# Feed-forward gate and up products with high and low rows as one 512-column operand, and a third of the modulation rows in the second block

## The reference

```python
h = x                                            # first_block, DEPTH = 2
for layer in range(2):
    h = h + mixer(rms_norm(h, mix_norm[layer]))  # layer 0: gated linear recurrence; layer 1: stick-breaking attention
    z = rms_norm(h, ffn_norm[layer])
    gu = z @ ffn_w_in[layer]                     # (256, 1024) @ (1024, 2 * 2816)
    h = h + (silu(gu[:, :2816]) * gu[:, 2816:]) @ ffn_w_out[layer]
x = rms_norm(h, final_norm)
# second_block
mod = silu(c) @ w_ada + b_ada                    # 6 vectors of 1024: shifts, scales, gates
x = x + g1 * attentions(rmsnorm(x) * (1 + sc1) + sh1)
x = x + g2 * mixture_of_32_experts(rmsnorm(x) * (1 + sc2) + sh2)
out = rmsnorm(x)
```

## Time and profile before

| | |
|---|---|
| median of 3 runs | 1275.25 us (1275.18 to 1276.27) |
| the profiled execution, span from first to last instruction | 1277.6 us |
| mean granted clock of PE | 0.953 |
| PE busy | 1116.7 us (87% of the span), 9331 matmuls |
| DVE busy | 685.3 us (54%) |
| ACT busy | 421.0 us (33%) |
| DMA | 362.48 MB, mean 284 GB/s |

### The profile page before, as it was taken

One profiled execution on the slowest core, in us unless ns is written; L12 is line 12 of the kernel. 1 busy time (PEld: TensorE's weight loads), 2 busy tenths in 40 slices (PEclk: granted clock), 3 DMA queues, 4 the chain that ended last, 5 costly groups with the idle time before them and its releaser, 6 DMA issues.

```text
span 1277.6 us, 23118 instructions
## 1 busy us (share of the span) xinstructions
PE 1116.7 (87%) x9331; PEld 904.2 (71%) x9333; DVE 685.3 (54%) x1069; ACT 421.0 (33%) x532; POOL 32.8 (3%) x71
## 2 busy tenths in 40 slices
PE   9999999999999999999999999678766567666676
PEld 8999999999968999999998899533322233322232
DVE  5799988887445746557866767632112112112114
ACT  3775333345384433334644673410000000000001
POOL 0000000000000000001000000000000000000000
PEclk9999999999999999999999999889888888888889
DMA  9678988874530785550463336799999999999996
GB/s 347 225 262 301 342 299 302 305 261 158 176 128 1 263 311 198 173 174 2 179 225 132 133 141 239 305 378 416 428 427 430 427 428 430 427 430 427 428 430 259
DMA packets 99401, 362.48 MB, mean 284 GB/s; under 512 B 4160, under 2 KB 51664, under 8 KB 84112
## 3 DMA queue, kind: packets, MB, share of 16 engines
q1 hardware_dynamic: 95216, 335.06, 68.0%
q0 software_dynamic: 3984, 26.50, 5.3%
q10 hardware_dynamic: 144, 0.10, 0.0%
HBM read 360.58 MB, written 1.06 MB: 283 GB/s over the span
## 4 chain that ended last, share of the span: by engine, by line
PE 60%; DMA 23%; DVE 10%; ACT 3%; issue 2%; another core or an unknown queue 1%; SPq 0%; POOLq 0%; DVEq 0%; POOL 0%; ACTq 0%
DMA wbuf<-in_w_up 22%; PE ps L1897 16%; PE ps L1820 9%; PE ps L1783 8%; PE ps L2231 6%; PE ps L2107 4%; DVE parts L1107 3%; PE ps L1804 3%; PE ps L1829 2%; PE ps L2251 1%; PE ps L2281 1%; PE ps L1773 1%; PE ps L2014 1%; PE ps L1980 1%; DMA wbuf<-in_ffn_w_in 1%
## 5 line engine op out<-in xcount | busy, mean ns | idle before, releaser
L2231 PE MATMUL ps<-wbuf,big 128*32 128x256 f32 x2176 | 166.2, 470 | 109.4 <-DMA wbuf<-in_w_up 97.8
L1897 PE MATMUL ps<-big_parts,parts 128*128 128x256 f32 x2112 | 255.0, 282 | 1.4 <-DVE parts L1107 1.4
L1107 DVE TENSOR_TENSOR parts<-wbuf,parts 128x2048 fp32r<-128x2048 f32 x92 | 208.7, 2287 | 84.8 <-ACT parts L835 43.9
L1897 PEld LDWEIGHTS ps<-big_parts,parts 128*128 128x128 f32 x2112 | 252.3, 188 | 2.2 <-DVE parts L1107 1.4
L2231 PEld LDWEIGHTS ps<-wbuf,big 128*32 128x32 f32 x2176 | 85.5, 134 | 203.8 <-issue 98.1
L1693 DVE TENSOR_TENSOR big<-big,ps 128x128 f32<-128x128 f32 x33 | 9.5, 288 | 265.2 <-ACT big L1039 265.2
L1039 ACT ACTIVATE big<-ps 128x128 f32<-128x128 f32 x33 | 9.2, 278 | 415.7 <-PE ps L2231 415.7
L1820 PE MATMUL ps<-big_parts,parts 128*128 128x256 f32 x1088 | 132.9, 282 | 0.6 <-DVE parts L1107 0.6
L1820 PEld LDWEIGHTS ps<-big_parts,parts 128*128 128x128 f32 x1088 | 130.7, 189 | 0.8 <-DVE parts L1107 0.8
L1783 PE MATMUL ps<-parts_f,parts 128*128 128x256 f32 x704 | 98.4, 284 | 0.0
L1783 PEld LDWEIGHTS ps<-parts_f,parts 128*128 128x128 f32 x704 | 90.5, 192 | 0.1
(11 more groups left out here) (353 smaller groups left out, 1409.9 us busy)
## 6 DMA issues: line engine op xcount, KB each, us to landing
wbuf<-in_w_down SPq DMA_DIRECT2D x32, 2048.0 KB, 37.9
wbuf<-in_w_gate SPq DMA_DIRECT2D x31, 2048.0 KB, 32.6
wbuf<-in_w_up SPq DMA_DIRECT2D x31, 2048.0 KB, 37.1
wbuf<-in_ffn_w_in SPq DMA_DIRECT2D x44, 1024.0 KB, 12.1
wbuf<-in_w_ada POOLq DMA_DIRECT2D x24, 1024.0 KB, 8.6
wbuf<-in_ffn_w_out SPq DMA_DIRECT2D x22, 1024.0 KB, 5.1
wbuf<-in_w_in SPq DMA_DIRECT2D x10, 2048.0 KB, 8.8
wbuf<-in_attn_w_qkv SPq DMA_DIRECT2D x6, 2048.0 KB, 8.6
```

Of the source, the lines that this page charges most:

```text
L1107: nc.vector.tensor_tensor(lo, whole, hi.bitcast(F32), ALU.subtract).then_inc(done, 1)
L1897: ins = mm(ps[:, b, d * 256:(d + 1) * 256], w[pw][:, k, d * P:(d + 1) * P], h_part_of[px][:, k], start=(k == 0 and d == 0 and i == 0), sto ...
L2231: ins = mm(at, rows, gu_place[s][:, :, k, r * P:(r + 1) * P], start=(k == 0), stop=(k == KC - 1))
```

## The change

1. `half` makes two matmuls for each k and d instead of three. The first has the high weights and a moving operand of 512 columns, the 256 high and the 256 low rows of the same chunk (`h_both`, one access pattern over both regions). The second has the low weights and the 256 high rows. A column group d now has a bank of its own, with the sum of two products in its left half and the product with the low rows in its right half. Gate has banks 0 and 1 in every step, up has 2 and 3.
2. ACT copies the right halves to SBUF (`copy_low`), DVE adds the left halves to them (`sum_of_parts`) and then scales the sum from SBUF to SBUF. PE waits for the sum of the step before when it writes the banks again. In a step ACT copies gate's right halves first (in step 0 of a stage behind the split of the next gate weights and the norm root), and up's after silu.
3. The norm's sums of squares use bank 5 instead of 3.
4. Units 0 to 15 of the modulation stay in `ffn(0)`, one or two at a step (`ADA_FROM`). The other 16 rows of 128 x 1024 are loaded one by one by POOL into a free region of `big` once `wo1` is used, and `ffn(1)` takes two of them at the end of each step from 1 to 8 (`ada_row`). The row `c_row` is loaded and activated a second time. The small instructions that make the gains stand behind step 8 of `ffn(1)`. "ada" is free after 16 units.

```diff
 WARM_UP = 20
-SUM_BANK = (7, 3, 5, 3, 3, 2, 0, 4)
+SUM_BANK = (7, 5, 5, 5, 3, 2, 0, 4)
...
-ADA_FROM = tuple(range(2, ADA_UNITS - 1, 2))
+ADA_FIRST = 16
+ADA_ROWS = ADA_GROUP * (ADA_UNITS - ADA_FIRST)
+ADA_FROM = (2, 3, 5, 6, 8, 9, 10, 12, 13, 15, ADA_FIRST)
 
...
         X_AT_FFN = WORK + 2080
         h_part_of = [big_parts[:, X_AT_FFN + i * 2048:X_AT_FFN + (i + 1) * 2048].rearrange("p (k t) -> p k t", k=KC) for i in range(2)]
+        h_both = big_parts[:, X_AT_FFN:X_AT_FFN + 4096].rearrange("p (i k t) -> p k i t", i=2, k=KC)
...
-                eng.wait_ge(ada_used, ADA_UNITS)
+                eng.wait_ge(ada_used, ADA_FIRST)
             elif name == "qm":
...
+            for u in range(ADA_FIRST):
                 if u >= 2:
                     pool.wait_ge(ada_used, u - 1)
                 pool.dma_start(ada_place[u % 2], a["w_ada_2"][:, ADA_GROUP * u:ADA_GROUP * (u + 1), :]).then_inc(ada_loaded[u % 2], 16)
+            pool.wait_ge(o_done, KC)
+            pool.dma_start(c_row, a["c_2"].to_broadcast([P, D])).then_inc(c_in, 16)
+            wait_used(pool, "wo1")
+            for r in range(ADA_ROWS):
+                if r >= 2:
+                    pool.wait_ge(ada_used, ADA_FIRST + r - 1)
+                pool.dma_start(ada_row_place[r % 2], a["w_ada_2"][:, ADA_GROUP * ADA_FIRST + r]).then_inc(ada_loaded[r % 2], 16)
 
             pool.wait_ge(mod_ready, 2)
...
 
+                def copy_low(dst, b):
+                    nc.scalar.activation(dst.rearrange("p (d t) -> p d t", d=2), ps[:, b:b + 2, SEQ:], ACT.Copy).then_inc(ffn_copied, 1)
+
                 def step(s, n, loads, next_loads, before=True):
 
+                    act.wait_ge(ffn_g, n + 1)
+                    if before:
+                        copy_low(hid[:, s], 0)
                     if next_loads is not None:
-                        act.wait_ge(ffn_g, n + 1)
                         split_g(1 - s, next_loads)
                         if not before:
                             norm_root(2 * layer + 1)
+                            copy_low(hid[:, s], 0)
                     else:
-                        act.wait_ge(ffn_g, n + 1)
                         act.wait_ge(fo_loaded[s], 16 * loads)
                         nc.scalar.activation(fd_part_last[0], ffn_views(s)[2], ACT.Copy).then_inc(fd_hi, 1)
                         if layer:
                             hi_unit("km")
-                    act.wait_ge(ffn_gate_scaled, n + 1)
+                    act.wait_ge(ffn_gate_scaled, 2 * n + 2)
                     nc.scalar.activation(hid[:, s], hid[:, s], ACT.Silu).then_inc(ffn_silu, 1)
                     act.wait_ge(ffn_gu, n + 1)
+                    if before:
+                        act.wait_ge(ffn_hid, 4 * n)
+                    copy_low(up_scaled, 2)
                     if next_loads is None:
                         hi_unit("qm" if layer else "q0")
...
                 step(0, base, ffn_loads(layer, 0), ffn_loads(layer, 1), before=False)
+                if layer:
+                    act.wait_ge(c_in, 32)
+                    nc.scalar.activation(c_row, c_row, ACT.Silu).then_inc(silu_c, 1)
...
+            def ada_row(unit, r):
+                w = ada_row_place[r]
+                dve.wait_ge(ada_loaded[r], unit * 16 + 16 * (ADA_FIRST // 2 + 1))
+                at = unit * ADA_GROUP + (ADA_GROUP * ADA_FIRST + r)
+                nc.vector.scalar_tensor_tensor(out=w, in0=w, scalar=1.0, in1=c_row, op0=ALU.mult, op1=ALU.mult, accum_out=ada[:, bass.ds(at, 1)]).then_inc(ada_used, 1)
+
             def ada_unit(u):
...
 
+            def modulation():
...
+                def sum_of_parts(dst, b):
+                    return nc.vector.tensor_tensor(by_token(dst), ps[:, b:b + 2, 0:SEQ], by_token(dst), ALU.add)
+
                 def scale_gate(s, n):
-                    dve.wait_ge(ffn_g, n + 1)
-                    nc.vector.tensor_tensor(by_token(hid[:, s]), by_token(ps[:, 2 * s, :]), root, ALU.mult).then_inc(ffn_gate_scaled, 1)
-
-                def step(s, n, following=True, first=False):
+                    dve.wait_ge(ffn_copied, 2 * n + 1)
+                    sum_of_parts(hid[:, s], 0).then_inc(ffn_gate_scaled, 1)
+                    dve.wait_ge(ffn_gate_scaled, 2 * n + 1)
+                    nc.vector.tensor_tensor(by_token(hid[:, s]), by_token(hid[:, s]), root, ALU.mult).then_inc(ffn_gate_scaled, 1)
+
+                def step(s, n, following=True, first=False, unit=None):
                     if first:
...
-                    dve.wait_ge(ffn_gu, n + 1)
-                    nc.vector.tensor_tensor(by_token(up_scaled), by_token(ps[:, 2 * s + 1, :]), root, ALU.mult).then_inc(ffn_hid, 1)
-                    dve.wait_ge(ffn_hid, 2 * n + 1)
+                    dve.wait_ge(ffn_copied, 2 * n + 2)
+                    sum_of_parts(up_scaled, 2).then_inc(ffn_hid, 1)
+                    dve.wait_ge(ffn_hid, 4 * n + 1)
+                    nc.vector.tensor_tensor(by_token(up_scaled), by_token(up_scaled), root, ALU.mult).then_inc(ffn_hid, 1)
+                    dve.wait_ge(ffn_hid, 4 * n + 2)
                     dve.wait_ge(ffn_silu, n + 1)
                     nc.vector.tensor_tensor(hid[:, s], hid[:, s], up_scaled, ALU.mult).then_inc(ffn_hid, 1)
...
-                    nc.vector.tensor_copy(hid_part[s][0], hid[:, s]).then_inc(ffn_hid_hi, 1)
-                    subtract(hid_part[s][1], hid[:, s], hid_part[s][0], ffn_hid_hi, n + 1, ffn_hid_lo)
+                    dve.wait_ge(ffn_hid, 4 * n + 3)
+                    nc.vector.tensor_copy(hid_part[s][0], hid[:, s]).then_inc(ffn_hid, 1)
+                    subtract(hid_part[s][1], hid[:, s], hid_part[s][0], ffn_hid, 4 * n + 4, ffn_hid_lo)
                     if following:
                         split_u(1 - s, n + 1)
                         subtract(fd_part[1], ffn_views(s)[2], fd_part[0], fd_hi, n + 1, fd_lo)
...
                         for u in range(ADA_FROM[n], ADA_FROM[n + 1]):
                             ada_unit(u)
+                    if unit is not None:
+                        for r in range(ADA_GROUP):
+                            ada_row(unit, r)
 
                 if layer == 0:
                     for n in range(FFN_STEPS):
                         step(n % 2, n, following=n + 1 < FFN_STEPS, first=n == 0)
                     return
                 step(0, base, first=True)
+                dve.wait_ge(silu_c, 2)
                 with dve.Fori(0, (FFN_STEPS - 3) // 2) as j:
-                    step(1, 2 * j + base + 1)
-                    step(0, 2 * j + base + 2)
+                    step(1, 2 * j + base + 1, unit=2 * j)
+                    step(0, 2 * j + base + 2, unit=2 * j + 1)
+                modulation()
                 step(1, base + FFN_STEPS - 2)
                 step(0, base + FFN_STEPS - 1, following=False)
 
             ffn(0)
             add_and_lower(lambda b: add_bank(f"ffn0_{FFN_STEPS - 1}", b), 2, xq_part, lambda k: col(R_MIX + KC + k), FH_ATT, False)
-            ada_unit(ADA_UNITS - 1)
 
...
                         for d in range(2):
-                            for i, (px, pw) in enumerate(PART_PAIRS):
-                                ins = mm(ps[:, b, d * 256:(d + 1) * 256], w[pw][:, k, d * P:(d + 1) * P], h_part_of[px][:, k],
-                                         start=(k == 0 and d == 0 and i == 0), stop=(k == KC - 1 and i == 2), skip_group_check=True)
+                            columns = slice(d * P, (d + 1) * P)
+                            mm(ps[:, b + d, :], w[0][:, k, columns], h_both[:, k], start=(k == 0), stop=False, skip_group_check=True)
+                            ins = mm(ps[:, b + d, 0:SEQ], w[1][:, k, columns], h_part_of[0][:, k], start=False, stop=(k == KC - 1), skip_group_check=True)
                     return ins
 
-                def gate_up(slot, step, between=None, wait_rows=False):
+                def gate_up(step, between=None, wait_rows=False, evacuated=True):
                     pe.wait_ge(fg_lo, step + 1)
-                    half(fg_part, 2 * slot, wait_rows).then_inc(ffn_g, 1)
+                    if evacuated:
+                        pe.wait_ge(ffn_gate_scaled, 2 * step - 1)
+                    half(fg_part, 0, wait_rows).then_inc(ffn_g, 1)
                     if between is not None:
                         between()
                     pe.wait_ge(fu_lo, step + 1)
-                    half(fu_part, 2 * slot + 1, False).then_inc(ffn_gu, 1)
+                    if evacuated:
+                        pe.wait_ge(ffn_hid, 4 * step - 3)
+                    half(fu_part, 2, False).then_inc(ffn_gu, 1)
 
                 n = 2 * layer + 1
...
-                gate_up(0, base, sums_of_two, wait_rows=True)
-                gate_up(1, base + 1, root_read)
+                gate_up(base, sums_of_two, wait_rows=True, evacuated=False)
+                gate_up(base + 1, root_read)
```

47 lines of the change are left out of this document (22 added, 25 removed).

## The result

| | before | after |
|---|---|---|
| median | 1275.57 us (4 runs, 1275.18 to 1276.27) | 1287.71 us (4 runs, 1286.67 to 1288.35) |
| ratio | | 1.0082, 95% interval 1.0066 to 1.0099 |
| span of the profiled execution | 1277.6 us | 1286.6 us |

The change makes the kernel slower by 12.1 us between the medians (the interval of the ratio is 8.4 to 12.6). The forecast was 6.85 us, with 1285.5 as its upper end: right in sign, too small by nearly half.

The account below looks back on a forecast made before the run. PE bounds both feed-forward stages, busy throughout at 2.4 GHz. First block -2.7 us and second +9.55 sum to +6.85, made against the profiled 1277.6 but put onto the median: 1282.1 us; 8 in 10 range 1273.0 to 1285.5.

Parts of the forecast that it names:

- block 1: start: First feed-forward: two more scalings in DVE's queue make PE's second up half start later, +1.4 us.
- 18 halves: In each block 18 gate or up halves (48 matmuls before) run unhindered, each 0.15 us shorter: -2.7 us a block.
- clock: Fall to 1.2 GHz after idle, charged once, at step 4 of block 2: +1.7 us (bounds 0 and 3.4).
- end: Last step of each block: sums ready before PE asks in block 1, -1.4 us; hidden parts later in block 2, +1.35.
- block 2: start, chain: Second feed-forward: copy, sum and low split queued on ACT and DVE make up(1) late, +2.7 us.
- start, contention: Block 2 start: a pair of moved rows delays step 1's weights on DMA, +2.7 us (bounds 0 and 2.7).
- start, clock: Block 2 start: no charge for a clock fall, since PE waits for DVE behind gate(1) anyway.
- gate(4): Step 4 of block 2: two pairs of rows delay weights behind km and vm, +3.8 us wait (bounds 0 and 3.8).
- Part 1: Wide operand: one wide and one narrow matmul take 346.6 ns, three narrow 356; a half takes 5.54 us.
- Rival 3: Fixed part only 2.5 ns, or two-piece operand slower: halves 5.65 to 5.69 us, 1286 to 1287.4 us; chance 0.08.
- Rivals 1 and 2: 1: rows' transfers hidden, 1273.9 us, chance 0.14 in full; 2: weight load paces narrow matmul, 1270.5 us, chance 0.07.

Follow-up runs that it names:

- wide_alone: The changed kernel with all units of modulation rows back in the first block; ratio 1.0037 against the kernel before.
- kept_warm: The changed kernel with matmuls of no use put into PE's waits at both blocks' starts; ratio 1.0058 against the kernel before.
- hold_only: The changed kernel with POOL's rows held back until step 1's weights have landed; no ratio, block 2 took 183.90 us in one profile.
- rows_alone: The kernel before with the rows moved as in the change, three narrow matmuls kept; ratio 1.0055 against the kernel before.
- operand_in_two: The changed kernel with each wide matmul cut into two of 256 columns, same bank and weights; no ratio, block 2 took 190.12 us.
- no_contention: The changed kernel with POOL's rows held back as in hold_only and km and vm spread as in spread_only; ratio 1.0019 against the kernel before.
- spread_only: The changed kernel with km and vm each loaded behind a further pair of steps on SP's queue; no ratio, block 2 took 181.93 us.
- pair_forms: The changed kernel with a one-piece wide operand and, in block 2, both wide matmuls before both narrow; no ratio, pairs 351 and 349 ns.

## Why the prediction was right in sign and wrong in size

| term of the sum | forecast | measured |
|---|---|---|
| block 1: start | +1.4 | +1.39 |
| 18 halves | -2.7 | -1.4 |
| clock | none | +1.5 |
| end | -1.4 | -1.28 |
| block 2: start, chain | +2.7 | +2.0 (`wide_alone`) |
| start, contention | +2.7 | +2.6 |
| start, clock | none | +1.0 |
| `gate(4)` | +3.8 | +3.28 |
| clock | +1.7 | +1.6 |
| 18 halves | -2.7 | -1.3 |
| end | +1.35 | +1.24 |

**Wrong: the price of the pair (Part 1).** "16 such groups save 0.15 us a half": they save 0.08, and the 36 free halves win 2.7 us instead of 5.4. I took the wide matmul's 227.9 ns from a stage in which only wide ones follow each other, and the narrow one's 118.7 from narrow ones among themselves. In turn they cost 230.7 and 120.5. These 2.7 us are the largest miss. Rival 3 comes nearest with its time, and its reasons fall: the one-piece operand costs the same. By the Trainium skill's formula quoted in the prediction (TensorE: Matmul & The Clock Gate, "Back-to-back issue gap") a pair would take an estimated 325 ns; the trace has 351. That section of the Trainium skill gives it for a matmul by itself, and here each has a weight load.

**Wrong: the clock in the first block.** I asked for a fall only behind gaps near 4 us, and charged it at step 4 alone. In the profile of the kernel after the 2.09 us ahead of `up(1)` were enough, and cost 1.5; four kernels with the same wait had no fall (below), so the timed runs may have this term only in part.

**Right: the first block's start**, +1.39 us where 1.4 was forecast.

**Right in sum, partly by luck: the second block's start.** `up(1)` comes 5.67 us late, where 5.4 was forecast. The sum's place in the queues costs 2.0 us, not 2.7: in `wide_alone`, where no rows are moved, `up(1)` is at 21.11 us against 19.08 before. The contention is as forecast: `kept_warm` has `up(1)` at 23.75, 2.6 us more, at full clock. The last 1.0 us is the clock, which the prediction charged at nothing there because PE waits for DVE anyway. The slow `gate(1)` took 8.31 us, where `up(1)` follows 7.40 us behind `gate(1)` if it waits for DVE (`wide_alone`, `hold_only`). The errors of the chain, 0.7 too much, and of the clock, 1.0 too little, so nearly cancel. The split into waits was not as I wrote it either: the slow half took up the wait that `up(1)` would have had, and `hold_only` shows this second wait, 1.54, where the clock stayed up.

**Right: step 4 and the end of the second block**, 0.5 and 0.1 us too high. At step 4 the terms agree too. From SP's issue to ACT's start on the weights it took 28.41 us instead of 23.24, so two pairs of rows add 5.2 us where 5.4 was forecast:

```profile
456.47 0.37 SPq L537 DMA_DIRECT2D wbuf<-in_ffn_w_out  x1
```

**Right in size, wrong in cause: the end of the first block.** The -1.28 belong to the moved rows (`rows_alone` has -1.29, `wide_alone` +1.71).

Rivals 1 and 2 fell: the transfers aren't hidden, and a pair is far from 327 ns. With the two misses put right the sum is 6.85 + 2.7 + 1.5 = 11 us, and the rest of the 12.1 is within the interval.

## What to carry to other kernels

A price per instruction holds at best among its neighbours (and in `operand_in_two` not even there, 356 and 360 ns): take it from rows where the same two kinds follow each other, or keep both ends in the range. Whoever moves loads onto a second queue should look for the two or three places where an engine already waits for a load or just doesn't, not at the mean DMA share: 0.61 hid 8 us of loss here, and one wait of a queue and another order of two loads gave them back. When an evacuation grows by an operation, order the first and last step anew, for there it is not hidden. And a term may be right as a sum of wrong parts: a run that takes one part away, as `wide_alone` does, shows it.

## What I had not expected of the hardware

**The same wait, and the clock falls or doesn't.** Seven kernels have all but the same work up to here and the same wait, 1.95 to 2.12 us, ahead of the first block's `up(1)`. In three (after, `no_contention`, `hold_only`) 1.2 GHz follow for 3.4 us; in four (`wide_alone`, `spread_only`, `pair_forms`, `operand_in_two`) none. The first five microseconds behind the wait, in the kernel after and in `spread_only`:

```profile
119.20:124.20 5.00, 4.96 (x19) 4.34 (x20) 5.00 (x6) 0.38 (x1) 0.28 (x1) 0.66 0.35 87
```
```profile
119.50:124.50 5.00, 5.00 (x29) 4.39 (x30) 4.99 (x6) 0.32 (x1) 0.32 (x1) 1.00 0.37 90
```

19 matmuls started in the one, 29 in the other. `gate(2)` follows 12.9 us behind `up(1)` where it fell and 11.4 where it didn't. So the term is 0 or 1.5 us in one execution, and a single profile doesn't tell which is usual.

**The queues' shares.** From 419 to 425 us of the kernel after, with the first rows on POOL's queue (0.5 MB each in 4 KB packets, 7.2 us to land) and step 1's weights on SP's (1.0 KB packets); the counts have some packets of 4 bytes in them:

```profile
DMA packets 1499, 2.28 MB, mean 380 GB/s; under 512 B 48, under 2 KB 1242, under 8 KB 1498
...
q1 hardware_dynamic: 1210, 1.22, 59.5%
q0 software_dynamic: 288, 1.05, 44.4%
```

The prediction left POOL about two thirds; it had 44.4%, with one packet to four of SP's. The prediction says that the earlier trace rows agrees with the Trainium skill's rule quoted there, of rings that take turns packet by packet (DMA: Bandwidth & Descriptors, "Queues, rings and completion order"). That goes too far. By the profile's packets the turns aren't one for one, neither there (252 to 507) nor here (288 to 1210). But a packet in that section of the Trainium skill holds several descriptors, and no run here shows whether the profile's packets are the same thing, so the rule is neither borne out nor refuted. The delay of the weights was 2.48 us all the same, about the time of the rows' own 1.05 MB.

**One kernel's time spreads more on some chips.** The kernel before took from 1275.2 to 1276.3 us on the first chip, the 0.1% named at the start, and from 1273.7 to 1280.3, or 0.5%, in the 52 runs on the three later ones. Differences under 2 us were read from the traces' half starts, which repeat within 0.1 us, or from the ratios.
